# Granules in step behind a norm, a root by columns, a later scaling and an earlier rounding in a two-block transformer kernel

## What is computed

```python
x_lat = x_lat + gt1 * mix
x_lat = x_lat + gt2 * sq_relu_mlp(modulate(rms_norm(x_lat, g_norm2[i]), sh2, sc2), w_mlp1[i], w_mlp2[i])
```

```python
h = rmsnorm(x, norm_g)
proj = h @ w_in
oa = diff_attention(q, k, v, lam)
oa = rmsnorm(oa, attn_norm_g) * (1.0 - lam_init)
oa = oa.transpose(0, 2, 1, 3).reshape(bsz, s, A_WIDTH) * jax.nn.silu(az)
...
hb = rmsnorm(hb, mlstm_norm_g).transpose(0, 2, 1, 3).reshape(bsz, s, B_WIDTH)
hb = jax.nn.sigmoid(bo) * hb * jax.nn.silu(bz)
u = jax.nn.sigmoid(ga) * ya + jax.nn.sigmoid(gb) * yb
return x + u @ w_o
```

## Time and profile before

| | |
|---|---|
| median of three runs | 1895.59 us (1894.59, 1895.59, 1902.32) |
| the profiled execution | 1896.9 us, span 1895.1 us |
| mean granted TensorE clock | 0.968 |
| TensorE busy | 1788.4 us, 94% of the span (weight loads 77%) |
| VectorE, ScalarE, GpSimd busy | 1107.1 us (58%), 885.5 us (47%), 417.1 us (22%) |
| chain of work that ended last | TensorE 83%, VectorE 7%, ScalarE 3%, GpSimd 3% |
| HBM over the span | 134 GB/s |

### The profile page before, as it was taken

One profiled execution on the slowest core, in us unless ns is written; L12 is line 12 of the kernel. 1 busy time (PEld: TensorE's weight loads), 2 busy tenths in 40 slices (PEclk: granted clock), 3 DMA queues, 4 the chain that ended last, 5 costly groups with the idle time before them and its releaser, 6 DMA issues.

```text
span 1895.1 us, 28571 instructions
## 1 busy us (share of the span) xinstructions
PE 1788.4 (94%) x10804; PEld 1452.9 (77%) x10804; DVE 1107.1 (58%) x1955; ACT 885.5 (47%) x1773; POOL 417.1 (22%) x832
## 2 busy tenths in 40 slices
PE   4999999899999998989899989999999899989998
PEld 2453454588888885747899989888899898878898
DVE  3327841687777533383555577566556585674555
ACT  2227631433333333472555566565554564664542
POOL 1014201000000001141000025065451161374430
PEclk8799989899999998999899989999999899999999
DMA  8321631255545530301455533532345335332351
GB/s 306 104 89 46 221 133 45 89 178 178 178 178 178 178 89 26 133 1 45 166 184 184 179 134 102 189 124 101 129 163 183 139 102 178 135 134 90 134 183 64
DMA packets 139876, 255.27 MB, mean 135 GB/s; under 512 B 14926, under 2 KB 21724, under 8 KB 139612
## 3 DMA queue, kind: packets, MB, share of 16 engines
q1 hardware_dynamic: 138742, 251.16, 38.2%
q0 software_dynamic: 704, 2.10, 0.3%
q10 hardware_dynamic: 294, 0.18, 0.0%
HBM read 252.38 MB, written 1.05 MB: 134 GB/s over the span
## 4 chain that ended last, share of the span: by engine, by line
PE 83%; DVE 7%; ACT 3%; POOL 3%; issue 2%; SPq 1%; DMA 1%; ACTq 0%; DVEq 0%; POOLq 0%
PE ps L1161 18%; PE ps L1163 17%; PE ps L1162 17%; PE ps L1170 10%; PE ps L1283 2%; PE ps L1045 2%; PE ps L1309 2%; PE ps L1375 1%; PE ps L1295 1%; PE ps L1377 1%; PE ps L1376 1%; PE ps L1072 1%; PE ps L1135 1%; SPq L817 1%; PE ps L1455 1%
## 5 line engine op out<-in xcount | busy, mean ns | idle before, releaser
L1564 ACT ACTIVATE big_r<-ring 128x1024 fp32r<-128x1024 f32 x198 | 209.3, 1058 | 395.0 <-PE ps L1163 386.3
L1988 DVE TENSOR_TENSOR big_r<-ring,big_r 128x1024 fp32r<-128x1024 f32 x198 | 246.3, 1245 | 240.1 <-ACT big_r L1564 240.1
L1162 PE MATMUL ps<-big_r 128*128 128x256 f32 (+1 forms) x1120 | 374.4, 334 | 0.0
L1161 PE MATMUL ps<-hT_r,big_r 128*128 128x256 f32 (+1 forms) x896 | 293.6, 328 | 10.9 <-DVE big_r L1997 10.6
L1163 PE MATMUL ps<-hT_r,big_r 128*128 128x256 f32 (+1 forms) x896 | 285.9, 319 | 0.0
L1162 PEld LDWEIGHTS ps<-big_r 128*128 128x128 f32 x1120 | 215.5, 192 | 19.5
L904 POOL TENSOR_TENSOR sq<-sq 128x256 f32<-128x256 f32 (+1 forms) x30 | 36.6, 1219 | 776.0 <-ACT sq L1524 776.0
L1170 PE MATMUL ps<-hT,ring 128*128 128x512 f32 (+1 forms) x544 | 191.4, 510 | 11.0 <-ACT hT L1585 9.2
L1161 PE MATMUL ps<-big_r 128*128 128x256 f32 (+1 forms) x592 | 195.8, 331 | 1.4 <-DVE big_r L2146 1.4
L1161 PEld LDWEIGHTS ps<-hT_r,big_r 128*128 128x128 f32 x896 | 175.4, 196 | 27.4 <-issue 11.8
L1163 PE MATMUL ps<-big_r 128*128 128x256 f32 (+1 forms) x592 | 194.8, 329 | 0.0
(11 more groups left out here) (298 smaller groups left out, 4019.1 us busy)
## 6 DMA issues: line engine op xcount, KB each, us to landing
ring<-in_w_in SPq DMA_DIRECT2D x42, 2048.0 KB, 7.9
ring<-in_w_mlp SPq DMA_DIRECT2D x32, 2048.0 KB, 7.8
ring<-in_w_mod SPq DMA_DIRECT2D x24, 2048.0 KB, 8.1
ring<-in_w_out SPq DMA_DIRECT2D x4, 2048.0 KB, 8.6
ring<-in_w_out_a SPq DMA_DIRECT2D x4, 2048.0 KB, 8.5
ring<-in_w_out_b SPq DMA_DIRECT2D x4, 2048.0 KB, 8.1
ring<-in_w_o SPq DMA_DIRECT2D x4, 2048.0 KB, 8.1
ring<-in_w_in SPq DMA_DIRECT2D x12, 256.0 KB, 5.0
```

The lines of the kernel that those rows point to most:

```text
L1161: mm(b[:, 0:T], w_hi[:, k, :], hi(k), start=(k == 0), stop=False)
L1162: mm(b[:, 0:T], w_hi[:, k, :], lo(k), start=False, stop=False)
L1564: act_fn(hi, raw, ACT.Copy).then_inc(hi_ready, 1)
L1988: V.tensor_tensor(lo, raw, hi.bitcast(F32), ALU.subtract).then_inc(lo_ready, 1)
```

## The change

Four parts.

1. **Two granules side by side.** `split_products_in_step` computes the first two granules behind a norm together: for each chunk six matmuls into two banks. It is used in the MLP of both layers (granules 0 and 1 of `up`) and in the second block (`aq0` and `aq1`). It waits until both granules are rounded, and at the norms a third granule is rounded earlier: in the MLP it has a pair of buffers of its own (`"third"`), and in the second block `hi_to` and `lo_to` of the fourth granule (number 3) stand ahead of the norm's chunks on ScalarE and ahead of `lam` on VectorE. `split_by` counts one more granule for the first two of the MLP. In `run_units` the mean squares of `aq0` and `aq1` move behind the third unit.
2. **The root by columns.** `root_of_mean` also has 16 instructions, but each takes its scalars as columns. The two columns (a head's two tiles of 128 tokens) alternate, and `await_all_but(n)` waits for all but the last n instructions instead of for all. `root_ready` now counts two per head.
3. **The scaling later.** In an odd step ScalarE now runs `projected(first)` ahead of the scaling (L1816), not behind it.
4. **A rounding ahead of the gates' wait.** ScalarE rounds the fourth `bv` granule ahead of `gabs_ready`.

```diff
+        buffers = {("mlp", "third"): pair(over(3)), ("b", "h"): ...
-            phase(("mlp", i), granules_of(i), lambda j: ("mlp", j % MLP_BUFS))
+            phase(("mlp", i), granules_of(i), lambda j: ("mlp", "third" if j == 2 else (j + (j > 2)) % MLP_BUFS))
...
-            return min(n + 1 + (MLP_BUFS if key[0][0] == "a" else B_BUFS), gran_cap[n])
+            if key[0][0] == "a":
+                return min(n + 1 + MLP_BUFS + (key[1] == "up" and key[2] < 2), gran_cap[n])
+            return min(n + 1 + B_BUFS, gran_cap[n])
...
+            def counted(ins):
+                chain[0] += 1
+                ins.then_inc(pool_chain, 1)
+
+            def await_all_but(n):
+
+                pool.wait_ge(pool_chain, chain[0] - n)
...
                     pool.wait_ge(ms_ready, 4 * NH2 * l + 2 * p + 2)
-                    link(nc.gpsimd.tensor_scalar(x, ms, 1.0 / P, EPS, ALU.mult, ALU.add))
-                    link(nc.gpsimd.tensor_scalar(y.bitcast(I32), x.bitcast(I32), -0.5, ROOT_SEED, ALU.mult, ALU.add))
-                    link(nc.gpsimd.tensor_scalar(x, x, -0.5, None, ALU.mult))
-                    for _ in range(3):
-                        link(nc.gpsimd.tensor_tensor(ms, y, y, ALU.mult))
-                        link(nc.gpsimd.tensor_tensor(ms, ms, x, ALU.mult))
-                        link(nc.gpsimd.tensor_scalar(ms, ms, 1.5, None, ALU.add))
-                        link(nc.gpsimd.tensor_tensor(y, y, ms, ALU.mult))
-                    nc.gpsimd.tensor_tensor(y, y, r, ALU.mult).then_inc(root_ready, 1)
+                    counted(nc.gpsimd.tensor_scalar(y, ms, 1.0 / P, EPS, ALU.mult, ALU.add))
+                    counted(nc.gpsimd.tensor_scalar(x, ms, -0.5 / P, -0.5 * EPS, ALU.mult, ALU.add))
+                    await_all_but(1)
+                    counted(nc.gpsimd.tensor_scalar(y.bitcast(I32), y.bitcast(I32), -0.5, ROOT_SEED, ALU.mult, ALU.add))
+                    await_all_but(0)
+                    for it in range(3):
+                        if it == 2:
+                            await_all_but(0)
+                            counted(nc.gpsimd.tensor_tensor(r, r, y, ALU.mult))
+
+                        for c in range(2):
+                            if 0 < it < 2:
+                                await_all_but(1)
+                            counted(nc.gpsimd.tensor_scalar(ms[:, c:c + 1], y[:, c:c + 1], y[:, c:c + 1], x[:, c:c + 1],
+                                                            ALU.mult, ALU.mult))
+                        for c in range(2):
+                            if it < 2:
+                                await_all_but(1)
+                                counted(nc.gpsimd.tensor_scalar(y[:, c:c + 1], ms[:, c:c + 1], 1.5, y[:, c:c + 1], ALU.add,
+                                                                ALU.mult))
+                            else:
+                                await_all_but(1 - c)
+                                nc.gpsimd.tensor_scalar(y[:, c:c + 1], ms[:, c:c + 1], 1.5, r[:, c:c + 1], ALU.add,
+                                                        ALU.mult).then_inc(root_ready, 1)
...
-                    if 0 <= j - MS_LAG < n and units[j - MS_LAG][1] == "norm":
+                    if in_step and j in (1, 2):
+
+                        for name, _, _ in units[0:2 * (j - 1)]:
+                            mean_squares(tag, name)
+                    elif 0 <= j - MS_LAG < n and units[j - MS_LAG][1] == "norm":
...
+            def split_products_in_step(n0, hi, lo, T):
+
+                keys = [granules[n0 + g][2] for g in range(2)]
+                banks = [start_bank(key) for key in keys]
+                pe.wait_ge(lo_ready, n0 + 2)
+                for k in range(KC):
+                    await_chunk(k)
+                    for g in range(2):
+                        w_hi, w_lo = gran_bufs[n0 + g]
+                        b = banks[g][:, 0:T]
+                        mm(b, w_hi[:, k, :], hi(k), start=(k == 0), stop=False)
+                        mm(b, w_hi[:, k, :], lo(k), start=False, stop=False)
+                        last = mm(b, w_lo[:, k, :], hi(k), start=False, stop=(k == KC - 1))
+                        if k == KC - 1:
+                            fill(last, keys[g])
...
-                        if name == "up":
+                        if (j, m) == (0, 0):
+                            split_products_in_step(n, lambda k: h_hi[:, k, t0:TOK], lambda k: h_lo[:, k, t0:TOK], TOK - t0)
+                        elif (j, m) == (0, 1):
+                            continue
+                        elif name == "up":
...
-                    split_product(gran_of[(tag, name, 0)], h_hi_at, h_lo_at, SEQ)
+                    if name == "aq0":
+                        split_products_in_step(gran_of[(tag, name, 0)], h_hi_at, h_lo_at, SEQ)
+                    elif name != "aq1":
+                        split_product(gran_of[(tag, name, 0)], h_hi_at, h_lo_at, SEQ)
...
-                        hi_to(first_gran["mlp", i] + MLP_BUFS)
+                        hi_to(first_gran["mlp", i] + MLP_BUFS + 1)
...
                 reciprocal_root((tag, "n1"), P, SEQ, D)
+                hi_to(first_gran["b", l] + 3)
...
-                hi_to(first_gran["b", l] + 3)
                 run_units(tag, units_b())
...
                 hi_to(split_by((tag, "bif")))
+                hi_to(gran_no[("bv", l, 0), 3] + 1)
                 act.wait_ge(gabs_ready, l + 1)
...
+                    for name, c in first:
+                        projected(name, c)
                     p, odd = divmod(step - 5, 2)
                     if 0 <= p < 2 * NH2 and not odd:
 
                         key = (tag, "o", p)
-                        act.wait_ge(root_ready, 2 * NH2 * l + p + 1)
+                        act.wait_ge(root_ready, 4 * NH2 * l + 2 * p + 2)
...
                         drain(last, key)
-                    for name, c in first:
-                        projected(name, c)
...
-                        lo_to(g0 + MLP_BUFS)
+                        lo_to(g0 + MLP_BUFS + 1)
...
+                lo_to(first_gran["b", l] + 3)
                 await_drained(dve, (tag, "lam"))
```

More of the change, by code:

```diff
@@ L526, in program @@
         norms = rounded_view("nt", [P, KC, P])[:, :, :], rounded_view("rstd", [P, KC, P])[:, :, :]
-        buffers = {("b", "h"): (hT_r[:, :, SEQ:SEQ + P], hT_r[:, :, SEQ + P:TOK]), ("b", "end"): pair(over(7)),
+        buffers = {("mlp", "third"): pair(over(3)), ("b", "h"): (hT_r[:, :, SEQ:SEQ + P], hT_r[:, :, SEQ + P:TOK]), ("b", "end"): pair(over(7)),
                    ("b", "spare"): spare, ("b", "norms"): norms, ("b", "mqk"): pair(over(4))}
@@ L1074, in run_units @@
             def run_units(tag, units, main, tail=()):
-                n = len(units)
+                n, in_step = len(units), tag[0] == "b"
                 for j in range(n + ROT_LAG):
```

## The result

The changed kernel took 1945.3 us (median of 4 runs, 1941.19 to 1949.39) against 1897.4 us before (four runs, the three above and one more): ratio 1.025, 95% interval 1.0215 to 1.0284. That is 48 us more, where 17.5 were forecast and 1932 was the upper end.

The account below looks back on a forecast made before the run. TensorE, busy 94% of the span, was taken as the bound, losing time to waits and half clock. Terms -11.6 (norms), -3.9 (gates), +38.0 (scaling) and -5 (clock) gave +17.5 us: 1913 us, range 1901 to 1932.

Parts of the forecast that it names:

- Clock: TensorE's clock in the heads: one drop per layer, 2 us in all, against 7 us that go, so -5.
- if half clock follows many of these waits: Sign of being wrong: half clock behind many value-product waits, where one drop per layer was taken.
- Rival B: Heads: the clock falls at a third of 24 stalls, adding some 20 us, 1933 us; chance 0.14.
- The scaling later: Heads: 24 value products each wait about 2.08 us for ScalarE; 53.5 us in sum, net +38 us.
- Two granules in step: Behind the norms: six matmuls per chunk make TensorE dense while chunks arrive; 11.6 us gained, bounds 4 and 14.
- rival C: Norms: the clock rises no sooner and one rounding is late; only 4 of 11.6 us come, 1921 us; chance 0.12.
- The rounding ahead of the gates' wait: Gates: the wait at the fourth `bv` granule goes, twice; 3.9 us gained, bounds 0 and 3.9.
- The root by columns: GpSimd root in the heads: 8 levels instead of 16, 3.5 us instead of 6.0, buying little here.
- Rival A: Heads: the new wait is hidden and the kernel faster, 1860 us with no stalls at all; chance 0.13.
- Rival D: Heads: stalls of 1.4 to 1.8 us at the value products, the sum about nothing; chance 0.05.

Follow-up runs that it names:

- e5_fill: The changed kernel with its head granules on two PSUM banks, plus 32 small unused matmuls ahead of each of 24 value products: 1920.6 us, against 1955.8 without the matmuls.
- e1_scale_back: The changed kernel with ScalarE's scaling back ahead of the step's first granule, nothing else undone: 1884.9 us, ratio 0.9922 to the kernel before.
- e6_two_banks: The changed kernel with value products alternating between banks 3 and 7, and granules among the heads on banks 5 and 6: 1861.9 us, ratio 0.98 to before.
- e8_two_banks_old_root: The changed kernel with value products alternating between two banks and the root on GpSimd as before: 1854.7 us, ratio 0.9761 to the kernel before.
- e2_scale_only: The kernel before, with only the scaling moved behind the step's first granule: 1965.8 us, ratio 1.0357 to the kernel before.
- e9_two_banks_back: The changed kernel with value products alternating between two banks, the old root, and the scaling back in its earlier place: 1864.7 us, ratio 0.9811 to before.

## Why the prediction was wrong

*The step that failed is **Clock***: "I take one drop per layer, 2 us in all, against the 7 us that go: -5." Measured were 26 us more lost than before. The prediction had the mechanism in hand and left it small. It read from four waits that 2.9 us lowered the clock once of two times and 1.3 us never, and put the new waits of 2.1 to 2.7 us on the harmless side, with nothing in the rows to say so. 11 of 22 of them lowered it, for 1.7 to 3.5 us each. e5_fill shows that it was these waits. The prediction had named this as a sign of being wrong: "if half clock follows many of these waits". Rival B had this form with a third of the waits and 0.14 as its chance, and gave 1933. With +26 in place of the -5 the prediction's sum is 17.5 + 31 = +48.5 us, which is what the runs gave (+48; the profiled executions, without the 3.0 us ahead of the first norm, are 47.3 apart).

*The scaling later* was right in mechanism and size: 24 waits, 12 per layer, 53.0 us where the sum had 53.5. A usual one is 1.90 to 1.91 us instead of 2.08, those behind a `bqk` product 2.36, as predicted four of them; a late tanh came six times, with 2.21, and not four. One per layer is 3.4 and 4.05 us, since the root there ended up to 2.04 us after ScalarE was free; the prediction had put it at about 1 us. So the total fits better than its parts: the usual waits are shorter than predicted, these two longer.

*Two granules in step*: 11.6 predicted, 12.9 measured in the trace, each place within its bounds or 0.1 above (4.35, 3.04, 2.98, 2.5 against 4.9, 2.3, 2.2, 2.2). The clock rose at 5.7 us or a little later, where 5 were taken. No cost of what went with it is seen (0.7 us elsewhere in the whole account): rival C is out.

*The rounding ahead of the gates' wait*: 3.9 predicted, 4.5 measured, which is above its upper bound of 3.9.

*The root by columns* was wrong, though it carried no part of the sum. From first to last instruction it took 4.5 to 7.4 us (mean 5.8 of all 32 heads), not 3.5, and before 4.4 to 6.5 (mean 5.7). The same head (p = 11) before, in the middle of its chain, and then after:

```profile
1373.35 0.20 POOL L984 TENSOR_TENSOR rn<-rn 128x2 f32<-128x2 f32 x1
1373.63 0.19 POOL L981 TENSOR_TENSOR rn<-rn 128x2 f32<-128x2 f32 x1
1373.90 0.19 POOL L982 TENSOR_TENSOR rn<-rn 128x2 f32<-128x2 f32 x1
1374.18 0.21 POOL L983 TENSOR_SCALAR rn<-rn 128x2 f32<-128x2 f32 x1
1374.48 0.20 POOL L984 TENSOR_TENSOR rn<-rn 128x2 f32<-128x2 f32 x1
1374.75 0.19 POOL L981 TENSOR_TENSOR rn<-rn 128x2 f32<-128x2 f32 x1
```

```profile
1380.49 0.67 POOL L1001 TENSOR_SCALAR rn<-rn 128x1 f32<-128x1 f32 x2
1381.13 0.51 POOL L1006 TENSOR_SCALAR rn<-rn 128x1 f32<-128x1 f32 x2
1381.62 0.66 POOL L1001 TENSOR_SCALAR rn<-rn 128x1 f32<-128x1 f32 x2
1382.26 0.51 POOL L1006 TENSOR_SCALAR rn<-rn 128x1 f32<-128x1 f32 x2
1382.85 0.19 POOL L996 TENSOR_TENSOR stat<-stat,rn 128x2 f32<-128x2 f32 x1
```

An iteration of four linked instructions took 1.12 us (1373.63 to 1374.75). Two pairs on single columns with column scalars take 1.13 (1381.13 to 1382.26). The floor of 0.14 us per instruction, taken from a cast of 256 columns behind the root, was the wrong row: an instruction on one column lasts some 0.34 us with two column scalars (L1001) and 0.26 with one (L1006). The first pair of L1001 above, which waits for nothing between its two, lasts 0.67 us, and the second, where each waits for its own column, 0.66. So half as many levels gained nothing. The bound from above (6.0 us, the old root's time) would have been the better guess. The sum didn't hang on it, since the late scaling rarely waits for the root; e1_scale_back and e6_two_banks, each beside its twin with the old root, took 5 and 7 us longer, since there the root is waited for. The root by columns lasted 6.0 us in the mean there against 5.7, and 6.4 against 6.1.

*Rival A* (faster) is out: the waits were not hidden. Its sum of what there was to gain, 1860 us without stalls, is close to what e6_two_banks measured (1861.9). Rival D (waits of 1.4 to 1.8 us) is out too: none of the 24 is under 1.90.

## What to carry to other kernels

A drain that is moved behind another engine's product must be counted from the end of that product, and if its bank is the only one of its kind each move costs a wait on TensorE: look for a second bank first. Here two banks turned the same change from a loss of 48 us into a kernel of 1861.9 us (e6_two_banks). With the root as before as well it took 1854.7 us (e8_two_banks_old_root), 2.4% below before and the fastest of all. Waits of TensorE of 1.9 to 2.4 us among dense work cost a further 1.25 us of full clock each on average in the changed kernel (27.4 us over 22), so waits of this size are to be priced at half as much again or more until a trace shows otherwise, and one of 0.6 us at itself. When the levels of a chain are cut, compare start to start of the old and the new instruction forms, not with the gap behind an unrelated one.

## What the runs showed of the hardware

- The same wait doesn't always do the same to the clock. In the changed kernel the twelve waits of either layer, 26.8 and 26.2 us long in all, went with 24.1 and 10.3 us lost; in e2_scale_only, 26.8 us long in each, with 20.6 and 20.5. It isn't shown that this is what spreads the runs of one kernel (1941 to 1949 us): of the kernels without such waits, e8_two_banks_old_root spreads by 1.7 us and e9_two_banks_back by 8.9.
- Over the eight profiled kernels with one bank and no filling matmuls, 1.7 us or more of full clock were lost in the window behind a value product's wait in 20 of 22 cases after 2.8 to 4.2 us, in 50 of 90 after 1.9 to 2.4, and in none of 32 after 0.4 to 1.7.
- Work that nobody uses can pay: 768 small matmuls on TensorE ahead of 24 waits made the kernel 35 us faster than its control, since the granted clock of the first layer's stretch rose from 0.90 to 0.99.
- GpSimd's instruction on one column with two column scalars lasted about 0.34 us, in pairs of 0.66 (L1001), where those on two columns without them lasted 0.19 to 0.20 us.
